# Products of the identity with ones on TensorE, ahead of the transposes at the crossings of a four-kind transformer stack

## Chip, cores and metric

The kernel runs on one core of a Trainium2 chip. The metric is the time of one execution on the device in microseconds, the median of three runs for the kernel before.

## What is computed

The input x is 256 tokens by 1024 features in float32. Four layers follow, each of an FFN, a mixer and a second FFN, with an RMS norm ahead of each and another behind it, then a fifth layer of another make with no norm behind its parts:

```python
for layer in range(DEPTH):                       # DEPTH = 4
    g = norm_g[layer]
    ff = swiglu(rmsnorm(h, g[0]), ffn_w_in[layer, 0], ffn_w_out[layer, 0])
    h = h + 0.5 * rmsnorm(ff, g[1])
    u = rmsnorm(h, g[2])
    ...
    h = h + rmsnorm(m, g[3])                     # m: the mixer of u
    ff = swiglu(rmsnorm(h, g[4]), ffn_w_in[layer, 1], ffn_w_out[layer, 1])
    h = h + 0.5 * rmsnorm(ff, g[5])
```

The mixers are sliding-window attention (swa, layers 0 and 3, with an output bias), gated linear attention (gla, layer 1) and a recurrence (rwkv, layer 2). Layer 4 is `x = x + 0.5 * swiglu(...)`, `x = x + hybrid_mixer(...)`, `x = x + 0.5 * swiglu(...)`, and a last RMS norm. The FFN's inner width is 2816. All weights are float32 in DRAM.

## The kernel before, in words

A list of stages is built by `network` and `joined`: "ffn", "proj" (a matrix product by column chunks), "cross", "turn", "attention" and "mixer". `build` writes every engine's instructions stage by stage, each engine in its own queue, with semaphores between them. Behind each stage every engine drains and signals (`barrier`), and where `passes` says so it doesn't wait for the others.

**Products.** Weights are loaded by SyncE into four buffers `raw`, then split into two parts of a rounded type (fp32r): ScalarE writes `high` (`split_high`, L303), VectorE writes `low = raw - high` (`split_low`, L307). The activations are split in the same way into `x_parts`, and a product is the sum of three (high by high, high by low, low by high), summed in PSUM. In an FFN (`ffn_pe`) unit q makes block q of gate and up (L372, L373, into `pair_bank[q % 2]`), then adds block q-1 to the output (L385 to L387, into the four `out_banks`). Unit 0 has no output part and ends in a drain of TensorE. A "proj" makes its products at L520.

**A crossing** ("cross") joins the norm behind one part with the norm ahead of the next. Its data is two tiles of 128 tokens by 1024. In `cross_act` and `cross_dve`, by turns: ScalarE sums the squares of the output (L594), takes a root (L597), VectorE multiplies by the gain (L645; with a bias it adds it first, L679, and then L682), takes the reciprocal (L654), and adds to h (L655; L658 where nothing is normed behind the part); then ScalarE squares h, and VectorE writes y = h / rms (L672), signalling `y_ready` once per tile. In `cross_pe`, TensorE waits for each tile's y and transposes its 8 blocks of 128x128 by the identity (L736) into `out_banks`; behind every second block of tile 1 it signals `x_turned`. ScalarE multiplies by the gain column and writes the high part (L630), VectorE the low part (L703), and the next stage's first product waits for `x_low`, block by block. Behind an FFN, VectorE puts the split of the next weight tile (L307) between y and the low parts (`splits_first`). Behind a mixer, GpSimd splits one tile once y is ready (`split_early_pool`, L283, L285).

There are 14 crossings with transposes. `tile_early` is true for the 13 of them that have a stage ahead (an FFN or a "proj" into the output): TensorE passes the barrier ahead of them without a wait. `post_gained` is true where the output is normed behind the part, which is all but the two within layer 4; of the 11 others, the two behind swa have a bias. `gate_bank[1]` is the first half of `pair_bank[1]`. `ident` is a 128x128 identity and `ones` a 128x128 tile of ones, both float32.

Of the kernel before, what the change touches and what calls it, by code (L numbers as in the profile page):

```python
# [11 lines left out]
P = 128  # L12
# [12 lines left out]
ARRIVAL = 64  # L25
CH = 256
UNROLL = 4
LOOPS = (FB - 2) // UNROLL - 1
MIX = 15518

# [60 lines left out]
def build(nc, io, out, stages):  # L91
# [7 lines left out]
    count = {}  # L99
# [39 lines left out]
    with ctx:  # L139
        def sb(name, shape, dt=F32):  # L140
            return ctx.enter_context(nc.sbuf_tensor(name, shape, dt))
# [17 lines left out]
        ident = sb("ident", [P, P])  # L159
        ones = sb("ones", [P, P])  # L160
# [12 lines left out]
        gate_bank = [b[:, 0:512] for b in pair_bank]  # L173
# [71 lines left out]
        def ends_in_tiles(st):  # L245
            return st.kind == "ffn" or st.kind == "proj" and st.dest == "out"

        def tile_early(st):
            return st.kind == "cross" and st.turn and st.at > 0 and ends_in_tiles(stages[st.at - 1])
# [48 lines left out]
        def split_high(act, u, w, turn=0, lo=0, count=1):  # L298

            act.wait_ge(arrived[u % RAW], ARRIVAL * (u // RAW + 1) + ARRIVAL * turn)  # L300
            if u >= SPLIT:
                act.wait_ge(weights_used, u - SPLIT + 1 + UNROLL * turn)
            nc.scalar.activation(high[u % SPLIT][:, lo:w], raw[u % RAW][:, lo:w], ACT.Copy).then_inc(high_ready, count)  # L303

        def split_low(dve, u, w, turn=0, lo=0, count=1):
            dve.wait_ge(high_ready, u + 1 + UNROLL * turn)
            nc.vector.tensor_tensor(low[u % SPLIT][:, lo:w], raw[u % RAW][:, lo:w],  # L307
                                    high[u % SPLIT][:, lo:w].bitcast(F32), ALU.subtract).then_inc(weights_split, count)
# [18 lines left out]
        def load_unit(sp, u, parts, turn=0):  # L327
            if u >= RAW or not isinstance(turn, int):
                sp.wait_ge(weights_split, u - RAW + 1 + UNROLL * turn)
            for n, (dst, src) in enumerate(parts):  # L330
# [23 lines left out]
        def ffn_pe(pe, st):  # L354
            def unit(q, turn=0):
# [5 lines left out]
                else:  # L361
                    pe.wait_ge(weights_split, u + 1 + UNROLL * turn)
                if q < FB:
                    if f + q >= 2:
                        pe.wait_ge(hidden_ready, f + q - 1 + UNROLL * turn)
                    for n in range(2):
# [28 lines left out]
            unit(1)  # L395
            with pe.Fori(0, LOOPS) as i:
                for k in range(UNROLL):
                    unit(2 + k, i)
            for q in range(2 + LOOPS * UNROLL, FB + 1):
                unit(q)  # L400

        def ffn_act(act, st):
            def unit(q, turn=0):
                if q < FB:
                    split_high(act, st.u0 + q + 1, SLOT, turn, lo=IN_W if q + 1 == FB or q == 0 and split_early(st) else 0)
                    if q == FB - 1 and follower(st) is not None:
                        split_early_high(act, follower(st))
                    act.wait_ge(gate_up_ready, st.nth * FB + q + 1 + UNROLL * turn)
                    if st.nth * FB + q >= 1:
                        act.wait_ge(hidden_ready, st.nth * FB + q + UNROLL * turn)  # L410
                    halves = pair_bank[q % 2][:, :].rearrange("p (n s) -> p n s", n=2)
                    nc.scalar.activation(lows[:, :, :], halves[:, :, SEQ:2 * SEQ], ACT.Copy).then_inc(lows_copied, 1)  # L412
                    act.wait_ge(sums_ready, st.nth * FB + q + 1 + UNROLL * turn)
                    nc.scalar.activation(silu[:, :], sums[:, 0, :], ACT.Silu).then_inc(silu_ready, 1)  # L414
                else:
                    nc.scalar.activation(idle[:, :], ones[:, 0:1], ACT.Sqrt)
                    if next_unit(st.at) is not None:
                        split_high(act, next_unit(st.at), words(next_unit(st.at)))

            unit(0)  # L420
            unit(1)
            with act.Fori(0, LOOPS) as i:
                for k in range(UNROLL):
                    unit(2 + k, i)
            for q in range(2 + LOOPS * UNROLL, FB + 1):
                unit(q)

        def ffn_dve(dve, st):
            def unit(q, turn=0):
                if q < FB:  # L430
                    if q == 0 and early_by_pool(st):
                        dve.wait_ge(early_low, early_before(st) + 1)
                    split_low(dve, st.u0 + q + 1, SLOT, turn, lo=IN_W if q + 1 == FB or q == 0 and split_early(st) else 0)
                    if q == FB - 1 and follower(st) is not None:
                        split_early_low(dve, follower(st))
                    g = st.nth * FB + q
                    dve.wait_ge(lows_copied, g + 1 + UNROLL * turn)
                    halves = pair_bank[q % 2][:, :].rearrange("p (n s) -> p n s", n=2)
                    nc.vector.tensor_tensor(sums[:, :, :], lows[:, :, :], halves[:, :, 0:SEQ],  # L439
                                            ALU.add).then_inc(sums_ready, 1)  # L440
                    dve.wait_ge(silu_ready, g + 1 + UNROLL * turn)
                    nc.vector.tensor_tensor(hidden[:, :], silu[:, :], sums[:, 1, :], ALU.mult).then_inc(hidden_made, 1)  # L442
                    dve.wait_ge(hidden_made, g + 1 + UNROLL * turn)
                    if g >= 2:
                        dve.wait_ge(weights_used, st.u0 + q + UNROLL * turn)
                    nc.vector.tensor_copy(hid_h[q % 2][:, :], hidden[:, :]).then_inc(hidden_rounded, 1)
                    dve.wait_ge(hidden_rounded, g + 1 + UNROLL * turn)
                    nc.vector.tensor_tensor(hid_l[q % 2][:, :], hidden[:, :], hid_h[q % 2][:, :].bitcast(F32),  # L448
                                            ALU.subtract).then_inc(hidden_ready, 1)
                elif next_unit(st.at) is not None and not splits_first(stages[st.at + 1]):  # L450
                    split_low(dve, next_unit(st.at), words(next_unit(st.at)))

            unit(0)
            unit(1)
            with dve.Fori(0, LOOPS) as i:
                for k in range(UNROLL):
                    unit(2 + k, i)
            for q in range(2 + LOOPS * UNROLL, FB + 1):
                unit(q)
# [259 lines left out]
        def turn_pe(pe, st):  # L719
            for x, (t, g) in enumerate(turn_fills(st)):  # L720
# [7 lines left out]
                                               ident[:, :])  # L728
                last.then_inc(turned, 1)

        def cross_pe(pe, st):
            for t in range(NT):
                pe.wait_ge(y_ready, st.pre0 + t + 1)
                for k in range(KB):
                    at = (k % 2) * SEQ + t * P
                    ins = nc.tensor.transpose(out_bank[k // 2][:, at:at + P], y[:, t, k * P:(k + 1) * P], ident[:, :])  # L736
                    if t == NT - 1 and k % 2 == 1:
                        ins.then_inc(x_turned, 1)
# [200 lines left out]
        @block.tensor  # L939
        def _(pe):  # L940
            pe.wait_ge(ident_ready, 4)
            for s, st in enumerate(stages):
                if st.kind in ("ffn", "proj", "turn", "attention"):
                    {"ffn": ffn_pe, "proj": proj_pe, "turn": turn_pe, "attention": att_pe}[st.kind](pe, st)
                elif st.kind == "cross" and st.turn:
                    cross_pe(pe, st)
                elif st.kind == "mixer" and st.pe:
                    st.pe(env, pe)
                barrier(pe, "pe", s)
# [1940 lines left out]
```

## Time and profile before

| | |
|---|---|
| median of 3 runs | 3256.72 us (3252.83 to 3258.34) |
| the profiled execution | 3259.21 us |
| its span, first to last instruction | 3257.4 us |
| TensorE busy | 2929.2 us (90%), granted clock 0.941 over the span |
| VectorE busy | 1952.1 us (60%) |
| ScalarE busy | 1419.4 us (44%) |
| DMA | 471.49 MB, mean 145 GB/s |

Times in the trace count from the first instruction. A granted clock of 1.00 is 2.4 GHz and one of 0.50 is 1.2 GHz; a number between them is a mean over the stretch. A matmul's end is modelled: the next one starts before it, so its duration is longer than its share of TensorE's time, and what matters is the distance between starts.

### The profile page before, as it was taken

Reading aid. Unit: us, or ns where it says so; the run is one execution under the profiler, and the core shown is the slowest. Engines: PE = TensorE matmul, PEld = TensorE weight load, DVE = VectorE, ACT = ScalarE, POOL = GpSimd, SP = SyncE. Lnnn points to the kernel's source line nnn. Section 1 sums busy time; section 2 is a strip of 40 time slices with the busy share of each in tenths; the row PEclk is TensorE's granted clock in tenths of the full one; section 3 lists DMA queues with packets and bytes.
Section 4 is the critical chain, followed back from the end, with each engine's and each line's share of the span. In section 5 each row is a group of like instructions: output and inputs, shape, how many; then the busy total and the mean of one; then the engine's idle time right before and its main releaser. Section 6 shows DMA issues by size and latency. Waiting matters only on the chain.

```text
span 3257.4 us, 43781 instructions
## 1 busy us (share of the span) xinstructions
PE 2929.2 (90%) x17484; PEld 2560.8 (79%) x17484; DVE 1952.1 (60%) x2341; ACT 1419.4 (44%) x1779; POOL 33.4 (1%) x19
## 2 busy tenths in 40 slices
PE   8987899999899997857886999998799999989998
PEld 6876787878788786847874887887688787988887
DVE  5665666666566666555555566666566664655565
ACT  4454545444444544431211445445444544444444
POOL 0000000000000000000000000000000000000000
PEclk9997999999899998968996999999899999999999
DMA  8643565644465663410000665654365564652663
GB/s 245 195 125 94 178 193 162 195 131 149 134 193 166 196 196 105 138 39 1 1 1 22 183 191 162 194 172 123 115 191 179 171 190 135 198 161 97 192 184 95
DMA packets 625085, 471.49 MB, mean 145 GB/s; under 512 B 41441, under 2 KB 592737, under 8 KB 624948
## 3 DMA queue, kind: packets, MB, share of 16 engines
q1 hardware_dynamic: 620292, 460.01, 46.9%
q10 hardware_dynamic: 4656, 9.56, 0.9%
q8 instruction: 97, 1.59, 0.2%
q14 instruction: 40, 0.33, 0.0%
HBM read 466.63 MB, written 1.84 MB: 144 GB/s over the span
## 4 chain that ended last, share of the span: by engine, by line
PE 78%; DVE 12%; ACT 5%; issue 2%; DMA 1%; PEldq 1%; DVEq 1%; ACTq 0%; SPq 0%; PEld 0%
PE pair_bank L372 25%; PE pair_bank L373 13%; PE pair_bank L520 11%; PE out_banks L385 6%; PE out_banks L387 6%; PE out_banks L386 6%; PE out_banks L520 3%; DVE low L307 1%; DVE mix L2008 1%; ACT high L303 1%; PE pair_bank L1849 1%; PE pair_bank L1862 1%; PEldq L229 1%; PE pair_bank L1860 1%; DVE h L655 1%
## 5 line engine op out<-in xcount | busy, mean ns | idle before, releaser
L307 DVE TENSOR_TENSOR low<-raw,high 128x3072 fp32r<-128x3072 f32 (+2 forms) x328 | 935.2, 2851 | 769.3 <-ACT high L303 769.3
L372 PE MATMUL pair_bank<-x_parts,high 128*128 128x512 f32 x3520 | 1239.2, 394 | 10.9 <-DVE x_parts L703 8.4
L373 PE MATMUL pair_bank<-x_parts,low 128*128 128x256 f32 x3520 | 986.3, 280 | 0.0
L303 ACT ACTIVATE high<-raw 128x3072 fp32r<-128x3072 f32 (+2 forms) x328 | 774.4, 2361 | 340.4 <-PE out_banks L387 193.8
L372 PEld LDWEIGHTS pair_bank<-x_parts,high 128*128 128x128 f32 x3520 | 661.1, 188 | 167.0 <-issue 14.1
L373 PEld LDWEIGHTS pair_bank<-x_parts,low 128*128 128x128 f32 x3520 | 666.5, 189 | 9.4
L412 ACT ACTIVATE sq_scratch<-pair_bank 128x512 f32<-128x512 f32 x220 | 131.7, 599 | 583.0 <-PE pair_bank L373 583.0
L385 PE MATMUL out_banks<-high,hid_h 128*128 128x512 f32 x880 | 348.4, 396 | 4.0 <-DVE hid_l L448 4.0
L386 PE MATMUL out_banks<-low,hid_h 128*128 128x512 f32 x880 | 347.9, 395 | 0.0
L387 PE MATMUL out_banks<-high,hid_l 128*128 128x512 f32 x880 | 347.8, 395 | 0.0
L520 PE MATMUL pair_bank<-x_parts,high 128*128 128x256 f32 (+1 forms) x1232 | 242.1, 298 | 42.9 <-DVEq L229 30.4
L520 PE MATMUL pair_bank<-high,x_parts 128*128 128x256 f32 x1216 | 232.9, 289 | 10.9 <-DVEq L229 6.0
L520 PEld LDWEIGHTS pair_bank<-x_parts,high 128*128 128x128 f32 (+1 forms) x1232 | 204.5, 204 | 48.3 <-issue 40.6
L520 PEld LDWEIGHTS pair_bank<-high,x_parts 128*128 128x128 f32 x1216 | 196.2, 195 | 13.5 <-issue 7.4
L385 PEld LDWEIGHTS out_banks<-high,hid_h 128*128 128x128 f32 x880 | 165.2, 188 | 47.2 <-issue 8.1
L387 PEld LDWEIGHTS out_banks<-high,hid_l 128*128 128x128 f32 x880 | 165.3, 188 | 39.6
L386 PEld LDWEIGHTS out_banks<-low,hid_h 128*128 128x128 f32 x880 | 165.3, 188 | 29.5
L520 PE MATMUL pair_bank<-x_parts,low 128*128 128x256 f32 (+1 forms) x616 | 181.8, 295 | 0.0
L520 PE MATMUL pair_bank<-low,x_parts 128*128 128x256 f32 x608 | 174.1, 286 | 0.0
L439 DVE TENSOR_TENSOR sq_scratch<-sq_scratch,pair_bank 128x512 f32<-128x512 f32 x220 | 151.1, 687 | 29.9 <-ACT sq_scratch L412 24.5
L414 ACT ACTIVATE silu<-sq_scratch 128x256 f32<-128x256 f32 x220 | 91.9, 418 | 175.9 <-DVE sq_scratch L439 175.8
L442 DVE TENSOR_TENSOR hidden<-silu,sq_scratch 128x256 f32<-128x256 f32 x220 | 93.5, 425 | 112.0 <-ACT silu L414 112.0
(348 smaller groups left out, 3080.7 us busy)
## 6 DMA issues: line engine op xcount, KB each, us to landing
raw<-in_ffn_w_in_dram SPq DMA_DIRECT2D x352, 512.0 KB
raw<-in_ffn_w_out_dram SPq DMA_DIRECT2D x176, 512.0 KB
raw<-in_ffn_w_dram SPq DMA_DIRECT2D x132, 512.0 KB
raw<-in_w_in_dram SPq DMA_DIRECT2D x32, 1024.0 KB
raw<-in_gla_w_in_dram SPq DMA_DIRECT2D x12, 1024.0 KB
raw<-in_rwkv_w_rkv_dram SPq DMA_DIRECT2D x12, 1024.0 KB
raw<-in_swa_w_qkv_dram SPq DMA_DIRECT2D x10, 1024.0 KB
raw<-in_swa_w_o_dram SPq DMA_DIRECT2D x8, 1024.0 KB
```

Source lines behind the costliest of these rows:

```text
L303: nc.scalar.activation(high[u % SPLIT][:, lo:w], raw[u % RAW][:, lo:w], ACT.Copy).then_inc(high_ready, count)
L307: nc.vector.tensor_tensor(low[u % SPLIT][:, lo:w], raw[u % RAW][:, lo:w], high[u % SPLIT][:, lo:w].bitcast(F32), ALU.subtract).then_inc(we ...
L372: nc.tensor.matmul(o, H[:, w], x_parts[:, k, :], start=(k == 0), stop=False)
L373: last = nc.tensor.matmul(o[:, 0:SEQ], L[:, w], xh[:, k, :], start=False, stop=(k == KB - 1))
L385: nc.tensor.matmul(o, hid_h[b][:, tok], H[:, w], start=(q == 1), stop=False)
L386: nc.tensor.matmul(o, hid_h[b][:, tok], L[:, w], start=False, stop=False)
L387: last = nc.tensor.matmul(o, hid_l[b][:, tok], H[:, w], start=False, stop=(q == FB))
L412: nc.scalar.activation(lows[:, :, :], halves[:, :, SEQ:2 * SEQ], ACT.Copy).then_inc(lows_copied, 1)
L414: nc.scalar.activation(silu[:, :], sums[:, 0, :], ACT.Silu).then_inc(silu_ready, 1)
L439: nc.vector.tensor_tensor(sums[:, :, :], lows[:, :, :], halves[:, :, 0:SEQ], ALU.add).then_inc(sums_ready, 1)
L442: nc.vector.tensor_tensor(hidden[:, :], silu[:, :], sums[:, 1, :], ALU.mult).then_inc(hidden_made, 1)
L520: last = nc.tensor.matmul(o, a, b, start=(j == 0), stop=(j == len(terms) - 1))
```

## The change

Before the transposes of each of the 13 crossings, TensorE runs products of `ident` with the first column of `ones`, read 512 times, into `gate_bank[1]`. They are 12 where the output is normed, 16 where it has a bias too, and 4 where it isn't normed. Nothing reads the result, and no wait stands ahead of them.

```diff
@@ -25,6 +25,7 @@
 UNROLL = 4
+WARM_NORM, WARM_BIAS, WARM_PLAIN = 12, 4, 4
 LOOPS = (FB - 2) // UNROLL - 1
@@ -728,7 +729,14 @@
+        def keep_warm(count):
+
+            for _ in range(count):
+                nc.tensor.matmul(gate_bank[1][:, :], ident[:, :], ones[:, 0:1].to_broadcast([P, 512]), start=True, stop=True)
+
         def cross_pe(pe, st):
+            if tile_early(st):
+                keep_warm(WARM_NORM + WARM_BIAS * (st.post_gained and st.post.bias is not None) if st.post_gained else WARM_PLAIN)
             for t in range(NT):
                 pe.wait_ge(y_ready, st.pre0 + t + 1)
```

## Rows read from the trace of the kernel before

**Rows 1.** The page: busy time and share of TensorE; the chain that ended last.

```profile
PE 2929.2 (90%) x17484; PEld 2560.8 (79%) x17484; DVE 1952.1 (60%) x2341; ACT 1419.4 (44%) x1779; POOL 33.4 (1%) x19
...
PE 78%; DVE 12%; ACT 5%; issue 2%; DMA 1%; PEldq 1%; DVEq 1%; ACTq 0%; SPq 0%; PEld 0%
```

**Rows 2.** Groups by line, TensorE: busy us, mean ns | idle before, releaser.

```profile
L736 PE MATMUL out_banks<-ident,y 128*128 128x128 f32 x224 | 49.5, 411 | 92.7 <-DVE y L672 92.7
```

**Rows 3.** Timeline, crossing after an FFN: start us, us, engine, line, count, [idle, releaser].

```profile
205.24 0.39 PE L386 MATMUL out_banks<-low,hid_h 128*128 128x512 f32 x1
205.48 0.40 PE L387 MATMUL out_banks<-high,hid_l 128*128 128x512 f32 x1
...
211.66 0.75 DVE L672 TENSOR_SCALAR y<-h,rstd 128x1024 f32<-128x1024 f32 x1
...
212.47 3.67 PE L736 MATMUL out_banks<-ident,y 128*128 128x128 f32 x16 [6.60 <-DVE y L672]
...
213.12 0.75 DVE L672 TENSOR_SCALAR y<-h,rstd 128x1024 f32<-128x1024 f32 x1
213.78 2.28 DVE L307 TENSOR_TENSOR low<-raw,high 128x2048 fp32r<-128x2048 f32 x1
214.96 2.30 ACT L630 ACTIVATE x_parts<-out_banks,gain_columns 128x256 fp32r<-128x256 f32 x6 [2.08 <-PE out_banks L736]
215.99 1.26 DVE L703 SCALAR_TENSOR_TENSOR x_parts<-out_banks,gain_columns,x_parts 128x256 fp32r<-128x256 f32 x3
...
216.61 0.61 PE L520 MATMUL pair_bank<-x_parts,high 128*128 128x256 f32 x2 [0.47 <-DVE x_parts L703]
```

**Rows 4.** Windows of it: busy us by engine, granted clock, DMA share, GB/s.

```profile
206.00:210.00 4.00, 0.00 (x0) 0.00 (x0) 3.90 (x5) 1.82 (x5) 0.00 (x0) 1.00 0.00 0
210.00:217.00 7.00, 4.06 (x18) 3.69 (x19) 6.30 (x10) 4.82 (x12) 0.00 (x0) 0.51 0.01 2
```

**Rows 5.** Timeline, crossing behind swa, with a bias.

```profile
330.30 0.28 PE L520 MATMUL out_banks<-high,low 128*128 128x256 f32 x1
...
341.42 2.67 ACT L630 ACTIVATE x_parts<-out_banks,gain_columns 128x256 fp32r<-128x256 f32 x7 [2.08 <-PE out_banks L736]
342.36 1.66 DVE L703 SCALAR_TENSOR_TENSOR x_parts<-out_banks,gain_columns,x_parts 128x256 fp32r<-128x256 f32 x4 [2.04 <-ACT x_parts L630]
```

**Rows 6.** Timeline, crossing in layer 4, not normed behind the FFN, clock at 1.00.

```profile
2723.89 0.40 PE L387 MATMUL out_banks<-high,hid_l 128*128 128x512 f32 x1
...
2728.17 1.09 PE L736 MATMUL out_banks<-ident,y 128*128 128x128 f32 x8 [0.31 <-DVE y L672]
2728.71 3.02 ACT L630 ACTIVATE x_parts<-out_banks,gain_columns 128x256 fp32r<-128x256 f32 x8 [1.58 <-PE out_banks L736]
2730.23 3.22 DVE L703 SCALAR_TENSOR_TENSOR x_parts<-out_banks,gain_columns,x_parts 128x256 fp32r<-128x256 f32 x8
```

**Rows 7.** Timeline, first products of units 0 and 1 of two FFNs.

```profile
1081.17 0.47 PE L372 MATMUL pair_bank<-x_parts,high 128*128 128x512 f32 x1 [0.53 <-DVE x_parts L703]
...
1087.48 0.47 PE L372 MATMUL pair_bank<-x_parts,high 128*128 128x512 f32 x1 [0.26 <-issue]
...
2020.72 0.77 PE L372 MATMUL pair_bank<-x_parts,high 128*128 128x512 f32 x1 [0.46 <-DVE x_parts L703]
...
2027.61 0.47 PE L372 MATMUL pair_bank<-x_parts,high 128*128 128x512 f32 x1 [0.26 <-issue]
```

**Rows 8.** Line L2275, its records (ns min/median/max), and two of its products in the timeline.

```profile
L2275 PE MATMUL pair_bank<-mix x16: 590/592/668, 2978.4 to 2997.1; 128*128 128x512 f32 x16
...
2978.42 1.88 PE L2275 MATMUL pair_bank<-mix 128*128 128x512 f32 x4
```

**Rows 9.** Windows with f32 products alone: the rwkv mixer, then L2021 and L2022.

```profile
1490.00:1500.00 10.00, 8.67 (x66) 7.53 (x66) 5.66 (x12) 2.06 (x6) 0.00 (x0) 1.00 0.00 0
1758.00:1774.00 16.00, 15.97 (x16) 3.87 (x16) 6.91 (x6) 1.35 (x2) 0.00 (x0) 0.50 0.00 0
```

## The prediction

> **What bounds the kernel now.** I read the page first: TensorE is busy for 2929 of 3257 us and holds 78% of the chain that ended last, so a microsecond in which TensorE's own work comes later is, as a rule, a microsecond of time [rows 1]. Next the groups by line: of TensorE's idle time, 92.7 us stand before the transposes of L736, and VectorE's y of L672 ends them [rows 2]. That is 14 crossings, 13 of which get the new products. Then one crossing in order of time, after an FFN [rows 3]. The last product ends at 205.88 (205.48 + 0.40); call this E. VectorE and ScalarE normalize, y of tile 0 is ready at 212.41 = E+6.5, y of tile 1 at 213.87 = E+8.0. TensorE transposes 16 blocks, ScalarE starts the high parts at 214.96 = E+9.1, VectorE the low parts at 215.99 = E+10.1, and the first product of the next stage follows 0.62 us later. Behind an FFN, VectorE's split of a weight tile (213.78 + 2.28 = 216.06) ends just as the low parts start: the transposes are then not the last thing waited for. The windows show what the change is about: the clock stands at 1.00 in the first 4 us of the wait and at 0.51 in the next 7 [rows 4], so transposes and, at times, the first products run at the lower level (1.2 GHz instead of 2.4).
>
> **What a warm clock is worth.** Two terms. (a) Transposes: cold, 16 of them with a wait inside take 3.67 us [rows 3]; warm, 8 take 1.09 [rows 6], so one follows the other after 0.12 us (1.09 less some 0.27 of the last one's own, over 7). The high parts start 0.72 us after tile 1's transposes begin when cold (y of tile 1 at 213.87, 0.37 us of the last of tile 0 behind it) and 0.54 us after when warm (2728.17 to 2728.71, [rows 6]). About 0.2 us a crossing, and behind an FFN nothing, since the split covers it. (b) First products: an FFN's unit 0 took 6.31 us where the clock was already up (1081.17 to 1087.48) and 6.89 where it came up 1.8 us late (2020.72 to 2027.61) [rows 7]. Two more crossings look like the latter (539 and 884 us), and one (2343 us) has a sixth of it: 1.9 us in all. In the other crossings the clock is back within 0.3 us of the first product. The whole prize is 3 to 4 us, 0.1% of the time.
>
> **What the products cost.** The diff queues 12 products behind each normed crossing (9 of them), 16 where the output has a bias (2: the swa layers), 4 where nothing is normed on the way out (2, in layer 4). TensorE takes its queue in order, so the transposes wait for the last of them, needed or not. Everything therefore hangs on the time of one product of ident with ones, both plain f32, 512 columns wide. The trace has no such product of these operands, but it has the same form: L2275, 128x128 with 128x512, f32 and not fp32r. The loop there issues 8 products and the trace shows 16 records, two for each, at 592 ns [rows 8]; four records (two products) take 1.88 us with a tail of 0.59 behind the last start, so 0.43 us a record and **0.86 us a product**, at full clock, the weight loads hidden. The products in an FFN of the same width are fp32r, and one starts 0.24 us after the other (205.24 to 205.48, [rows 3]): a price of 3.6 times less that doesn't hold here. Against this stands the Trainium skill (TensorE: Matmul & The Clock Gate, "Back-to-back issue gap"), which gives the gap by columns alone, 0.216 us for 512 of them when warm; by it twelve products would take an estimated 2.6 us and fit the wait. The f32 rows say four times that, and the rows decide.
>
> Bounds for a record: 0.43 from below (none that wide is faster), 0.50 from above if the weight load showed partly. I take 0.43. The first product starts after a drain; an FFN has such a drain between units 0 and 1, with 0.26 us of idle TensorE [rows 7]. I take 0.26, between 0 and 0.55 (the weight loader's gap at that place, seen as an upper end).
>
> **The sum, crossing by crossing**, clock up throughout.
> - 12 products: the transposes may begin at E + 0.26 + 24 x 0.43 = E+10.6, 4 us after y of tile 0 and 2.6 us after that of tile 1. So all 16 go through at once: tile 1's begin at E+11.5 (8 x 0.12 later), the high parts at E+12.1 (+ 0.54), the low parts at E+13.0 (+ 0.94, as 341.42 to 342.36 in [rows 5], where no split is in the way). Before: E+10.1. Later by 2.9 us; times 9 is 26.1. The split on VectorE that covered this place is long done.
> - 16 products: E (330.58) + 0.26 + 32 x 0.43 = E+14.0, low parts at E+16.5. Before 342.36 = E+11.8 [rows 5]. Later by 4.7; times 2 is 9.4.
> - 4 products: E + 0.26 + 8 x 0.43 = E+3.7, low parts at E+6.1. Before, 2730.23 = E+5.9 (E is 2724.29) [rows 6], and alike in the other, at 3054 us. Later by 0.2 each, 0.4 in all.
> - First products warm: minus 1.9.
>
> Sum: 26.1 + 9.4 + 0.4 - 1.9 = **34 us later**. What is queued behind: ScalarE's high parts, VectorE's low parts and the barrier of both, so the weight splits of the next stage move along, and nothing fills the gap. Loads hide nothing either: SyncE's are let go by VectorE's splits, which are not later at the crossing, and DMA is at 0.00 to 0.01 there [rows 4], with tiles already in. GpSimd's early split starts with y and ends earlier against the products. The bank written (gate_bank[1]) has no reader in this stretch, so I cost it at nothing. The later stages are bound by TensorE or by chains that start with these products; a delay passes through one to one.
>
> The profiled execution took 3259.2 us (span 3257.4), 2.5 above the median shown, 3256.7. Its own time becomes 3293; against the median, **3291**.
>
> **Rivals.**
> 1. **The products fit (0.09).** If a product costs what the FFN's cost (0.24 us), or half of the f32 price (one record, 0.43), twelve end at E+3.1 or E+5.4 and sixteen at E+7.1 at most, before y at E+6.5 and E+8.3. Then only the prize is left: 3253, which is within 0.2%, about what can be told from no change. This is the case on the other side; it decides at a product of 0.52 us (6.5 - 0.26 over 12). For it: the product is a new operand pair, one of them a single column read 512 times. Against it: the count of records in L2275.
> 2. **The clock falls under the products (0.08).** Busy isn't enough: for 16 us TensorE ran f32 products of 512 columns (L2021 and L2022, 15.97 of 16 us busy) and the clock stayed at 0.50 [rows 9]. The Trainium skill has it that activity releases the throttle (same page, Part 1: The HAM clock gate); this stretch doesn't agree. One record started 1.0 us after the other there (16 in 16 us). If identity and ones count as little work, the clock falls some 3 us after E as it does now; 7 records are through, 17 more at 1.0 us end at E+20.5, and cold transposes bring the high parts to E+23: 14 us later, times 9, some 20 times 2 with a bias and 1 each for the short ones, 168 us in all, 3425; at 0.85 us a record (twice 0.43) 3395. For it the row named and a matrix that is zero off its diagonal; against it, half of those records have 32 rows only, and f32 products with all rows, 87% busy, had 1.00 at 1490 to 1500 [rows 9].
> 3. **Something takes the delay in (0.03).** Then a loss of under 20 us. I see no such cover.
>
> Forecast: 0.80. A range of 3276 to 3318 holds it: below, products starting at once (13 x 0.26 = 3.4), the scatter of the runs shown (3) and some cover; above, 0.50 us a record (9 x 24 + 2 x 32 + 2 x 8 = 296 records by 0.07, 21 us), a start at 0.55 (3.8) and no prize. The rivals lie outside it. **Chances:** faster by over 0.2% 0.02, since even the whole prize is 4 us against 6.5; within 0.2% 0.09; slower 0.89.
>
> **What would show it.** In the new profile: 296 records of 128x512 f32 at the new line, 592 ns each and 0.43 apart; TensorE's idle time before L736 gone (92.7 to under 20 us) and VectorE no longer named there; ScalarE's wait for L736 before the high parts up from 2.1 to 5 us after an FFN; clock 1.00 through the crossings; unit 0 at 6.3 us. I am wrong if a product has one record or 0.24 us, if the clock in the crossing is 0.50, or if the high parts start at E+9 as before.

## The result, and the profile after

The changed kernel takes 3291.65 us (median of 4 runs, 3290.44 to 3294.88) against 3256.53 us (4 runs): 35.1 us more, ratio 1.0111, 95% interval 1.0093 to 1.0128. The profiled execution took 3292.2 us with a span of 3290.3, 32.9 above the span before. Lines of the code behind the new function are 1 to 8 higher than before: L307 is now L308, L372 L373, L672 L673, L703 L704, L736 L744, and the new product is L735.

From the page, TensorE's busy time and the chain that ended last:

```profile
PE 3036.1 (92%) x17780; PEld 2595.5 (79%) x17780; DVE 1952.7 (59%) x2341; ACT 1419.5 (43%) x1779; POOL 33.1 (1%) x19
...
PE 82%; DVE 9%; ACT 4%; issue 2%; PEldq 1%; DMA 1%; DVEq 1%; ACTq 0%; SPq 0%; PEld 0%
```

TensorE is 107 us busier than in [rows 1], the other engines as busy as before, and TensorE's share of the chain rose from 78 to 82%, at the cost of VectorE and ScalarE: at the crossings, the chain no longer runs through the norms. Groups by line on TensorE and ScalarE show it again (busy us, mean ns | idle before, releaser):

```profile
L735 PE MATMUL pair_bank<-ones,ident 128*128 128x512 f32 x296 | 131.0, 597 | 1.4
...
L744 PE MATMUL out_banks<-ident,y 128*128 128x128 f32 x224 | 28.4, 283 | 11.1 <-DVE y L673 11.1
...
L631 ACT ACTIVATE x_parts<-out_banks,gain_columns 128x256 fp32r<-128x256 f32 x112 | 42.3, 490 | 61.5 <-PE out_banks L744 61.5
```

296 records for 148 products, two each. The 92.7 us for which the transposes waited for y [rows 2] are gone but for the program's first crossing, which has no new products (11.1), and a transpose takes 283 ns in the mean instead of 411. In their place ScalarE waits for the transposes.

Timeline of the crossing of [rows 3]:

```profile
206.55 0.40 PE L388 MATMUL out_banks<-high,hid_l 128*128 128x512 f32 x1
...
207.05 10.61 PE L735 MATMUL pair_bank<-ones,ident 128*128 128x512 f32 x24
...
212.74 0.75 DVE L673 TENSOR_SCALAR y<-h,rstd 128x1024 f32<-128x1024 f32 x1
...
214.19 0.75 DVE L673 TENSOR_SCALAR y<-h,rstd 128x1024 f32<-128x1024 f32 x1
214.86 2.28 DVE L308 TENSOR_TENSOR low<-raw,high 128x2048 fp32r<-128x2048 f32 x1
...
217.50 1.91 PE L744 MATMUL out_banks<-ident,y 128*128 128x128 f32 x16
218.85 3.02 ACT L631 ACTIVATE x_parts<-out_banks,gain_columns 128x256 fp32r<-128x256 f32 x8 [4.89 <-PE out_banks L744]
219.79 2.44 DVE L704 SCALAR_TENSOR_TENSOR x_parts<-out_banks,gain_columns,x_parts 128x256 fp32r<-128x256 f32 x6 [2.65 <-ACT x_parts L631]
```

E is 206.95. Both y are ready where they were, at E+6.5 and E+8.0 (212.74 + 0.75 = 213.49 and 214.19 + 0.75 = 214.94): the normalizing isn't disturbed. The transposes start at E+10.55, the low parts at E+12.84, where they had started at E+10.1. VectorE's split ended at 217.14 and then the engine waited 2.65 us. The windows of the crossing (busy us by engine, granted clock, DMA share, GB/s):

```profile
207.00:211.00 4.00, 3.95 (x9) 1.82 (x10) 3.84 (x5) 1.81 (x6) 0.00 (x0) 1.00 0.02 4
211.00:221.00 10.00, 8.99 (x37) 5.08 (x36) 6.65 (x11) 5.00 (x12) 0.00 (x0) 1.00 0.30 63
```

The change does what it is meant to do: the clock stays at 1.00, where it was 0.51 [rows 4]. Behind swa, with 16 products (E is 333.51):

```profile
333.62 14.06 PE L735 MATMUL pair_bank<-ones,ident 128*128 128x512 f32 x32
...
349.80 0.88 DVE L704 SCALAR_TENSOR_TENSOR x_parts<-out_banks,gain_columns,x_parts 128x256 fp32r<-128x256 f32 x2 [6.54 <-ACT x_parts L631]
```

Low parts at E+16.3, and at E+11.8 before [rows 5]. In layer 4 (E is 2757.93) they start at 2763.88, E+5.95, as before [rows 6]; in the other crossing of layer 4 they start 0.1 us later than before.

### The profile page after: what moved, and what is told of

Read it like the earlier page. It is cut to its first block, busy times and chain, and to the rows that moved or that the text cites. A ratio compares the mean times of both kernels' runs of the same rounds, so it can differ in the third digit from the quotient of the medians.

```text
span 3290.3 us, 44373 instructions
## 1 busy us (share of the span) xinstructions
PE 3036.1 (92%) x17780; PEld 2595.5 (79%) x17780; DVE 1952.7 (59%) x2341; ACT 1419.5 (43%) x1779; POOL 33.1 (1%) x19
## 4 chain that ended last, share of the span: by engine, by line
PE 82%; DVE 9%; ACT 4%; issue 2%; PEldq 1%; DMA 1%; DVEq 1%; ACTq 0%; SPq 0%; PEld 0%
PE pair_bank L373 25%; PE pair_bank L374 13%; PE pair_bank L521 11%; PE out_banks L386 6%; PE out_banks L388 6%; PE out_banks L387 6%; PE pair_bank L735 4%; PE out_banks L521 4%; DVE mix L2016 1%; PE pair_bank L1857 1%; PE pair_bank L1870 1%; ACT high L304 1%; PEldq L230 1%; DVE low L308 1%; PE pair_bank L1868 1%
## 5 line engine op out<-in xcount | busy, mean ns | idle before, releaser
L308 DVE TENSOR_TENSOR low<-raw,high 128x3072 fp32r<-128x3072 f32 (+2 forms) x328 | 935.2, 2851 | 770.1 <-ACT high L304 770.1
L373 PE MATMUL pair_bank<-x_parts,high 128*128 128x512 f32 x3520 | 1238.0, 394 | 16.1 <-DVE x_parts L704 13.5
L373 PEld LDWEIGHTS pair_bank<-x_parts,high 128*128 128x128 f32 x3520 | 660.4, 188 | 173.3 <-issue 21.5
```

What stands on the lines that cost most here:

```text
L373: nc.tensor.matmul(o, H[:, w], x_parts[:, k, :], start=(k == 0), stop=False)
```

## Experiments

My theory: the loss is time in TensorE's queue. A product is two records of 0.43 us each; what ends after the transposes could have begun is paid in full, and nothing else costs. The rivals: the products cost by being there (fetching, memory, PSUM), or another part than the type of the operands does; and for the clock, that what the products are decides whether it holds. Every edit is shown against the changed kernel, the last two runs aside, which repeat kernels unchanged. Every run is compared with executions of the kernel before that were made beside it; their median lay between 3253.65 and 3254.66 us.

### Seven, nine and two products

```diff
-WARM_NORM, WARM_BIAS, WARM_PLAIN = 12, 4, 4
+WARM_NORM, WARM_BIAS, WARM_PLAIN = 7, 2, 2
```

> Counts of 7, 9 and 2 products where the change has 12, 16 and 4. My theory (the loss is queue time of f32 products beyond y, 0.43 us a record, two records a product, the first one 0.10 us behind the last real product): they end at E+6.1, E+7.8 and E+1.8, all ahead of y (E+6.5, E+8.3, E+2.4), so the whole loss of 35 us goes and what is left is the clock's prize, 2 to 4 us under the kernel before: 3253 to 3255, clock 1.00 in the crossings, unit 0 of an FFN at 6.3 us, transposes 0.12 us apart. Rival (the products cost by being there: instructions fetched, PSUM or SBUF shared with VectorE and ScalarE): a part of the loss in proportion to the count stays, 7/12 of 35 = 20 us, 3277, and L673 ends later than E+6.54.

Measured: 3253.94 us (11 runs) against 3253.65 for the kernel before (21 runs), ratio 0.9996, interval 0.9987 to 1.0005. The whole loss is gone with five products of twelve taken away, so it is no cost per product: 20 us would have been left. The time lies in the range on record, 3253 to 3255, but that range was meant as 2 to 4 us under the kernel before, which took 3253.65 here: the loss went as expected, the gain didn't come. Its timeline, the same crossing:

```profile
206.18 6.29 PE L735 MATMUL pair_bank<-ones,ident 128*128 128x512 f32 x14
...
212.67 1.10 PE L744 MATMUL out_banks<-ident,y 128*128 128x128 f32 x8 [0.20 <-DVE y L673]
...
213.98 2.29 DVE L308 TENSOR_TENSOR low<-raw,high 128x2048 fp32r<-128x2048 f32 x1
214.12 1.09 PE L744 MATMUL out_banks<-ident,y 128*128 128x128 f32 x8 [0.35 <-DVE y L673]
214.66 3.02 ACT L631 ACTIVATE x_parts<-out_banks,gain_columns 128x256 fp32r<-128x256 f32 x8 [1.58 <-PE out_banks L744]
216.18 2.04 DVE L704 SCALAR_TENSOR_TENSOR x_parts<-out_banks,gain_columns,x_parts 128x256 fp32r<-128x256 f32 x5
```

The transposes wait for y again, and they are fast (8 in 1.1 us). But the low parts start at E+10.11 (E is 206.07), no earlier than before: VectorE's split ends at 216.27, as the prediction said. That holds in six of the seven crossings behind an FFN. In the seventh the split is short (0.28 us), and the low parts come earlier; the kernel before, then this run:

```profile
735.48 3.23 DVE L703 SCALAR_TENSOR_TENSOR x_parts<-out_banks,gain_columns,x_parts 128x256 fp32r<-128x256 f32 x8 [1.83 <-ACT x_parts L630]
...
733.49 3.23 DVE L704 SCALAR_TENSOR_TENSOR x_parts<-out_banks,gain_columns,x_parts 128x256 fp32r<-128x256 f32 x8 [1.33 <-ACT x_parts L631]
```

That is E+10.03 (E is 725.45) and E+9.52 (E is 723.97). In six of the 13 crossings the low parts are 0.5 us earlier in this way, 3.0 us in all, and the units 0 behind nine crossings are 1.9 us shorter together. The profile has these 4.9 us; the median of the runs doesn't, and why not is the matter of the last experiment.

### Twice the products

```diff
-WARM_NORM, WARM_BIAS, WARM_PLAIN = 12, 4, 4
+WARM_NORM, WARM_BIAS, WARM_PLAIN = 24, 8, 8
```

> Counts of 24, 32 and 8: twice those of the change. My theory: every product more is 0.86 us more of waiting, 9 x 12 + 2 x 16 + 2 x 4 = 148 products, 127 us above the change: 3419. Rival (the loss has another part than queue time, which doesn't grow, or the clock falls under long stretches of such products): under 3380, or over 3480 with a granted clock of 0.50 in the crossings.

Measured: 3421.05 us (2 runs), ratio 1.051 (1.0491 to 1.053). My theory said 3419. The span is 3418.6, 128.3 above the change's, and 128.3 / 148 is 0.867 us for a product more: two records of 0.43. The clock is 0.955 over the span, as in the change, and in no crossing does it fall, not under the 21 us of such products behind an FFN either.

### Operands of type fp32r, the same counts

```diff
-nc.tensor.matmul(gate_bank[1][:, :], ident[:, :], ones[:, 0:1].to_broadcast([P, 512]), ...
+nc.tensor.matmul(gate_bank[1][:, :], x_parts[:, 0, 0:P], x_parts[:, 1, :], ...
```

> Counts as in the change (12, 16, 4), but the operands are fp32r (blocks of x_parts, 128x128 with 128x512, in place of ident and ones); nothing else differs. My theory (the f32 type is what costs): one record a product, 0.24 us apart, twelve end at E+2.9 and sixteen at E+3.9, no transpose waits for them, and the loss is gone. TensorE is then idle for 3.6 to 4.4 us ahead of y, so the clock may fall or not: 3252 to 3257. Rival (the count or the 512 columns cost, whatever the type): 3280 to 3292.

Measured: 3259.83 us (11 runs), ratio 1.0020 (1.0011 to 1.0029), 6 us over the kernel before. The type was the price: twelve products take 3 us, and 29 of the 35 us go. (The edit changes the operands too, a tile in place of one column read 512 times. That this column is not what costs is shown by L2275 [rows 8], which reads whole tiles in f32 at the same 0.43 us a record.) The time is 3 us above the range that I expected; the trace names a place. Timeline and windows of the crossing (E is 205.95):

```profile
206.05 3.02 PE L735 MATMUL pair_bank<-x_parts 128*128 128x512 f32 x12
...
212.54 1.09 PE L744 MATMUL out_banks<-ident,y 128*128 128x128 f32 x8 [3.47 <-DVE y L673]
...
216.68 0.77 PE L521 MATMUL pair_bank<-x_parts,high 128*128 128x256 f32 x2 [0.72 <-DVE x_parts L704]
217.25 0.41 PE L521 MATMUL pair_bank<-x_parts,low 128*128 128x256 f32 x1
217.46 0.63 PE L521 MATMUL pair_bank<-x_parts,high 128*128 128x256 f32 x2
```

```profile
210.00:213.80 3.80, 1.09 (x8) 0.86 (x8) 3.10 (x6) 2.85 (x6) 0.00 (x0) 1.00 0.00 0
213.80:220.60 6.80, 5.89 (x26) 5.52 (x27) 5.65 (x11) 3.03 (x8) 0.00 (x0) 0.50 0.54 111
```

In the kernel before the clock fell 4 us after E and was back as the first product began. Here it falls 8 us after E and stays down for 4 us of products, three of which start every 0.64 us (217.46 to the next at 218.10) instead of every 0.36. Over 4 us that loses 1.8 us. In four crossings the low clock reached 3.7 us or more into the products; in the profile before, never more than 1.9. In two of the four it is an FFN's unit 0 that runs slowly, 7.8 and 7.9 us instead of 6.4. Four such places, at 1.5 to 1.8 us each, come to 6 to 7 us, the size of the loss. (The span of this profile, 3256.8, is not above that of the kernel before, 3257.4, but 7.2 above that of the run with 7, 9 and 2 products; the last experiment says why the first comparison misleads.) Twelve fast products, put right behind E, hold the clock over the part of the wait where nothing needs it and let it fall where it costs.

### Enough fp32r products to fill the wait

The products are those of the fp32r run, with other counts:

```diff
-WARM_NORM, WARM_BIAS, WARM_PLAIN = 12, 4, 4
+WARM_NORM, WARM_BIAS, WARM_PLAIN = 27, 8, 9
```

> As the fp32r run before (x_parts in place of ident and ones), with 27, 35 and 9 products where it had 12, 16 and 4, so that at 0.24 us each they end just ahead of y. That run was 6 us slower than the kernel before, though nothing waited for its products. My theory: its products end 3.4 us ahead of y, and the idle time behind them lets the clock fall later than in the kernel before, so that the cold stretch lies on the next stage's products and no longer on the wait. With the wait filled the clock stays at 1.00 to the end of the crossing and those 6 us go: 3249 to 3255. Rival (fp32r products from x_parts cost by themselves, by reading memory or writing PSUM beside VectorE): more products cost more, 3262 to 3268.

Measured: 3256.31 us (11 runs) against 3254.66 (23 runs), ratio 0.9999 (0.9990 to 1.0008), in two medians that differ by 1.6 us the other way: no difference. The time is 1 us above the range of my theory and far from the rival's. With more than twice the products of the run before, its 6 us are gone. Products don't cost by themselves, and the idle time behind them did. Timeline and window of the same crossing:

```profile
206.87 6.43 PE L735 MATMUL pair_bank<-x_parts 128*128 128x512 f32 x27
213.36 0.86 PEld L744 LDWEIGHTS out_banks<-ident,y 128*128 128x128 f32 x8 [0.49 <-DVE y L673]
```

```profile
213.00:221.00 8.00, 5.98 (x46) 5.25 (x45) 6.74 (x13) 3.77 (x11) 0.00 (x0) 1.00 0.40 82
```

### The same twelve fp32r products, late

The products are fp32r, 12, 16 and 4 of them; the arguments of `keep_warm` are left out here:

```diff
             if tile_early(st):
+                pe.wait_ge(h_ready, posts_before(st) + 1)
                 keep_warm(...)
```

> The first fp32r run (12, 16, 4 products) with one wait ahead of them, for h of tile 0, 4.0 us after E, so that the same products run in the 3 us up to y and the idle time lies ahead of them. They end at about E+7.0, which tile 1 can bear. My theory (where the idle time lies decides): the clock falls under the idle time and the transposes, as in the kernel before, or is back by the first products, and the 6 us are gone: 3250 to 3256. Rival (the products themselves cost those 6 us): 3258 to 3262 again.

Measured: 3264.60 us (6 runs), ratio 1.0036 (1.0022 to 1.0050): 12 us over the kernel before by the ratio, 10 by the medians. Both expectations missed. The crossing at 726 us (E is 726.25), timeline and window:

```profile
730.28 5.41 PE L735 MATMUL pair_bank<-x_parts 128*128 128x512 f32 x12 [4.03 <-DVE h L656]
...
735.53 1.91 PE L745 MATMUL out_banks<-ident,y 128*128 128x128 f32 x16
736.88 3.03 ACT L631 ACTIVATE x_parts<-out_banks,gain_columns 128x256 fp32r<-128x256 f32 x8 [3.62 <-PE out_banks L745]
737.82 3.22 DVE L704 SCALAR_TENSOR_TENSOR x_parts<-out_banks,gain_columns,x_parts 128x256 fp32r<-128x256 f32 x8 [3.38 <-ACT x_parts L631]
```

```profile
730.30:735.50 5.20, 5.20 (x12) 4.02 (x13) 3.44 (x7) 2.85 (x6) 0.00 (x0) 0.50 0.00 0
```

Behind 4 us of idle time the clock is down, so the products take 5.4 us instead of 3.0, end at E+9.3 instead of E+7.0, and hold the transposes up: low parts at E+11.6 instead of E+10.0. I had priced them at full clock. Added over the 13 crossings of this profile the low parts are 12.7 us later than in the profile before, which is the size of the loss. It is queue time again, with a price that the clock raises from 0.24 us a product to 0.44. The sum doesn't close in the profile: its span is only 2.4 us above that of the kernel before, since everything between the low parts of one crossing and the end of the products ahead of the next is 10 us shorter in it, added up. That nothing else costs is therefore likely, not shown.

### Nine, eleven and three products

```diff
-WARM_NORM, WARM_BIAS, WARM_PLAIN = 12, 4, 4
+WARM_NORM, WARM_BIAS, WARM_PLAIN = 9, 2, 3
```

> The change with counts of 9, 11 and 3. They end at E+7.9, E+9.6 and E+2.7, which is 1.3, 1.3 and 0.3 us after y of tile 0. My theory: the transposes of tile 0 may be that late at no cost, since those of tile 1 wait for a y 1.45 us later, and behind an FFN VectorE's split ends at E+10.1 anyway; low parts at E+10.1 and E+11.9, as before: 3252 to 3256, as with 7, 9 and 2. Rival (every microsecond beyond y is paid): 9 x 1.3 + 2 x 1.3 = 14 us more, 3268.

Measured: 3258.10 us (11 runs) against 3254.66, ratio 1.0007 (0.9998 to 1.0016), so between 1 us less and 5 us more; 14 are excluded. The median is 2 us above the range of my theory. In the same crossing (E is 205.99):

```profile
206.10 8.02 PE L735 MATMUL pair_bank<-ones,ident 128*128 128x512 f32 x18
...
213.96 1.91 PE L744 MATMUL out_banks<-ident,y 128*128 128x128 f32 x16
215.31 3.03 ACT L631 ACTIVATE x_parts<-out_banks,gain_columns 128x256 fp32r<-128x256 f32 x8 [2.30 <-PE out_banks L744]
216.25 2.05 DVE L704 SCALAR_TENSOR_TENSOR x_parts<-out_banks,gain_columns,x_parts 128x256 fp32r<-128x256 f32 x5
```

Tile 0's transposes start 1.4 us after their y and the low parts at E+10.26, 0.15 later than before. So behind an FFN with a long split the point from which a product is paid lies here, and not at y of tile 0. Where no long split is in the way (three crossings without a bias), the low parts were at E+9.5 with seven products and are at E+10.26 with nine: there 0.7 us is paid already, the 0.5 us that the warm transposes had gained and 0.2 more.

### Products with 32 rows

```diff
-nc.tensor.matmul(gate_bank[1][:, :], ident[:, :], ones[:, 0:1].to_broadcast([P, 512]), ...
+nc.tensor.matmul(gate_bank[1][:, :], ident[0:32, :], ones[0:32, 0:1].to_broadcast([32, 512]), ...
```

> Products of the change with 32 rows in place of 128 (ident[0:32], ones[0:32]), same counts and columns. The queue time of a product goes by its columns, so with a clock held at full the time is that of the change, 3288 to 3295. The rival to that, from the stretch of L2021 and L2022 that stayed at 0.50 though TensorE was busy: products with few rows don't hold the clock, it falls under them some 3 us after E, a record then takes 0.85 to 1.0 us, and the time is 3395 to 3425 with a clock near 0.5 in the crossings.

Measured: 3385.76 us (4 runs), ratio 1.0409 (1.0393 to 1.0426), 94 us over the change with the same number of instructions and columns. Timeline and windows of the crossing:

```profile
206.30 15.83 PE L735 MATMUL pair_bank<-ones,ident 32*128 32x512 f32 x24
222.06 3.19 PEld L744 LDWEIGHTS out_banks<-ident,y 128*128 128x128 f32 x16 [1.50 <-issue]
```

```profile
206.00:210.00 4.00, 3.90 (x10) 1.74 (x10) 3.63 (x4) 2.02 (x6) 0.00 (x0) 1.00 0.01 4
...
212.00:222.00 10.00, 10.00 (x12) 3.35 (x11) 3.86 (x4) 1.17 (x3) 0.00 (x0) 0.50 0.54 102
```

TensorE is busy for all of 10 us and the granted clock is 0.50. A record starts 0.85 us after the one before (12 in 10 us), twice 0.43. So the mechanism of the second rival exists, for these products of 32 rows, and those of the change, with 128 rows, don't meet it, although an identity is nearly all zeros too. The edit takes away rows and, with them, 96 of the 128 ones on the diagonal; which of the two the clock goes by is not separated here. The time is 9 us under the rival's range: the clock fell 3 us after E in some crossings, in most of them only 4 to 6 us after it, so fewer records ran at the low level.

### Both kernels once more

> The kernel before, unchanged, for a second profile and more runs. The profiles gave 7 us between it and the run with 7, 9 and 2 products, the medians none. If the first profile was a good sample, this one has a span of 3255 to 3259 and the clock's prize is real (5 us or so); if profiles scatter by some microseconds between executions of one kernel, its span is 3250 to 3254, with other cold stretches within the crossings and in the rwkv stage, and no prize can be told from profiles one by one.

> The run with 7, 9 and 2 products again, unchanged, beside the kernel before. If warm crossings are worth the 3 to 4 us of my prediction, its median is 2 to 5 us under that of the kernel before on this chip; if they are worth nothing that shows, it is within 2 us, as in the first run (3253.9 against 3253.7).

Measured beside another 23 runs of the kernel before (3254.59): the kernel before 3253.87 us, ratio 0.9996 (0.9988 to 1.0005), with a span of 3261.6 and a clock of 0.939 in its profile; 7, 9 and 2 products 3255.39 us, ratio 1.0004 (0.9995 to 1.0012), with a span of 3252.0 and a clock of 0.954. The profiles differ by 7.8 us the first time (3257.4 and 3249.6) and 9.6 the second, the medians by less than 2 us and not to the good of the warm kernel. So the second expectation of the last pair came true (within 2 us: nothing that shows), and the span of the kernel before lay in neither range expected for it. Its second profile has nearly the same stretches of low clock as the first up to 2700 us, and it is the longest of its 12 runs (3263.4). So its two profiled executions were longer than its usual one, and the prize read from them is too large.

The traces name one place, far from any crossing. In the rwkv mixer, from the first product of L1707 to that of L1729, the same 33 products take 17.8 us in both profiles of the kernel before and 14.3 in both of 7, 9 and 2 products. Windows of the first two profiles, the kernel before first:

```profile
1412.20:1430.00 17.80, 9.92 (x33) 7.73 (x34) 2.29 (x1) 7.74 (x17) 0.00 (x0) 0.58 0.01 3
...
1410.30:1424.60 14.30, 6.43 (x33) 5.34 (x34) 2.29 (x1) 7.74 (x17) 0.00 (x0) 0.80 0.09 21
```

The clock is 0.58 in the first and 0.80 in the second. It is not warm crossings that decide it: the changed kernel, with warm crossings, has 17.8 us too, and the two fp32r runs of twelve products, with a low clock in crossings, have 14.3. Of the 7.8 us between the first two profiles, 3.5 lie here, 3.0 at the low parts and 1.9 in the units 0 of the FFNs. Against this, the swa mixer of layer 3, from the end of the products ahead of one crossing to that ahead of the next, took 123.4 us at a clock of 0.88 in the first profile of the kernel before, and 125.1 at 0.86 and 127.2 at 0.85 in the two profiles of 7, 9 and 2: the low clock also moves about within the mixers. The mean clocks point the same way: of the 23 executions of the kernel before that stand beside the runs with 9 and with 27 products, the four with a mean clock of 0.940 or less are the four longest (3258 to 3263 us). Whether the 4.9 us won at the crossings are lost again in the mixers in a usual execution is not shown: those have a mean clock and no timeline.

## Why the prediction was right

The forecast was 3291, the measured median is 3291.65. By its steps:

- **Price of a product, 0.86 us, two records.** Right: 592 ns and 0.43 apart, 0.867 by the doubled run. The row of another line, of the same form and type, was worth more than the rule by columns alone; the fp32r run shows what that rule would have been right for.
- **Start, E+0.26.** Mis-sized: E+0.10 (207.05 against 206.95). The idle time between units 0 and 1, from which I took it, is longer than that behind the last product; why, no run shows.
- **Later by 2.9, 4.7 and 0.2 us a crossing.** Measured 2.7 (12.84 - 10.11) to 2.8, 4.5 (16.29 - 11.79) and 0 to 0.1; added over the 13 crossings of the two profiles, 33.9 us, for 35.9 in the sum. The difference is the earlier start, 13 times 0.15.
- **The clock's prize, 1.9 us off the sum, 3 to 4 in all.** The first products are right in the profiles: unit 0 of an FFN takes 6.3 to 6.5 us in the changed kernel, and the units are 1.9 us shorter together in the run with 7, 9 and 2. The transposes are mis-sized: 0.5 us, not 0.2, and in six crossings. I had counted the 0.72 us less 0.54, but not the 0.37 us for which tile 1 stands behind tile 0, and that goes too when the clock is up. In the medians nothing of it is found: three comparisons of warm crossings without a queue gave 0.9996, 0.9999 and 1.0004, with intervals that reach down to 4.2, 3.3 and 1.6 us less than the kernel before. This step is the one not borne out. It and the start, which I put too late, miss by about 2 us each in opposite ways, so that the sum is closer than its terms, and that is luck.
- **Clock held.** Right, on thin grounds: one window of f32 products at 1.00 stood against one at 0.50 [rows 9]. The 32-row run shows that the rival, read from L2021 and L2022, was a real one. Of its two prices, 0.85 us a record is what the low clock gives there, not 1.0.
- **Nothing takes the delay in; the split behind an FFN covers the transposes.** Right: the low parts of the crossings are 33.9 us later and the span is 32.9 longer, and behind an FFN the low parts start at E+10.1 with fast and slow transposes alike, in six crossings of seven. At 725 us the split is short, and there they gained 0.5 us.
- **First rival (the products fit).** It was false for the change. Its number for the case that they do fit, 3253, looks like the 3254 that fitting counts gave, but it stood for 4 us less than the kernel before, and they gave no difference. The point from which it decides was put at 0.52 us a product, by y of tile 0; behind an FFN with a long split the run with nine products shows 1.4 us more room, that is about 0.65.

No version tried beats the kernel before. The best, with the wait filled and no more, is equal to it.

## What to carry to other kernels

Work put into an idle engine's queue ahead of a wait is only free up to the moment at which its consumer would have been the last thing waited for; price one instruction from a row of the same form and type, multiply, and compare with that moment. Plain f32 products on TensorE cost 3.6 times those of fp32r of the same size here (0.867 us against 0.24). Before reading a small gain from two profiles, look at stretches that the change doesn't touch: here one of them differed by 3.5 us. Before warming a clock, work out what runs cold on the critical path: here it was some 4 us of 3257, of which the medians showed nothing, and filling half of the wait made things worse than filling none.

## What was not expected of the hardware

- Products of 32 rows kept TensorE busy without a gap and the granted clock fell to 0.50 under them; under products of 128 rows, of the same counts and columns, it stayed at 1.00, though their operands are zeros and ones as well.
- Products at the start of a wait, with 3.5 us of idle time behind them, moved the stretch of low clock 4 us later, onto real work: 6 us slower. Those at its end ran at the low clock themselves: 10 to 12 us slower.
- The same 33 products of the rwkv mixer took 17.8 us at a mean clock of 0.58 in some profiles and 14.3 at 0.80 in others, with warm and with cold crossings alike.
- Profiled executions of the kernel before took 3259.2 and 3263.4 us where its medians were 3256.5 and 3253.9, which is as much as the effect that I wanted to read from them.
